# A two-layer hybrid backbone on one core: another order of the scan's preparation, the norms and the transposes of the mixed heads

## The reference

```
u = modulated_norm(x) @ w_in                 # partitioned into the head groups
ssd  = rmsnorm((y_f + flip(y_b) + xh * d) * silu(z))
hy   = order-2 long convolution
ml   = head_norm(h_f + flip(h_b)) * sigmoid(o)
x    = x + gate * (concat(ssd, hy, ml) @ w_out)
x    = x + gate * moe(modulated_norm(x))     # top group, then top 2 of its 8 experts
```

## Time and profile before

| | us |
|---|---|
| Runs | 1514.76, 1512.43, 1507.62 |
| Median | 1512.43 |
| The profiled execution's own time | 1514.76 |
| Its span in the trace | 1512.8 |

### The profile page before, as it was taken

One profiled execution on the slowest core, in us unless ns is written; L12 is line 12 of the kernel. 1 busy time (PEld: TensorE's weight loads), 2 busy tenths in 40 slices (PEclk: granted clock), 3 DMA queues, 4 the chain that ended last, 5 costly groups with the idle time before them and its releaser, 6 DMA issues. The chain is left out here.

```text
span 1512.8 us, 20013 instructions
## 1 busy us (share of the span) xinstructions
PE 1242.1 (82%) x7740; PEld 830.7 (55%) x7740; DVE 633.8 (42%) x1275; ACT 315.8 (21%) x622; POOL 128.2 (8%) x144
## 2 busy tenths in 40 slices
PE   5899999998889668899868449999879488888880
PEld 1544548987668544555434246568767355454450
DVE  4424862055792542333212164844474522222223
ACT  3202112243333201131101122122522111111111
POOL 0000000000000011212111000000000111211210
PEclk9999999998999779998979779999989599899896
DMA  9633232244430539999989455341532489999982
GB/s 284 190 112 112 74 101 70 91 148 135 137 115 29 195 124 375 396 365 363 378 285 388 177 192 186 112 125 43 195 117 73 183 323 393 376 386 376 375 334 88
DMA packets 157910, 322.19 MB, mean 213 GB/s; under 512 B 27963, under 2 KB 117112, under 8 KB 141176
## 3 DMA queue, kind: packets, MB, share of 16 engines
q1 hardware_dynamic: 146424, 305.12, 56.6%
q0 software_dynamic: 11392, 15.77, 3.3%
HBM read 321.11 MB, written 21.23 MB: 226 GB/s over the span
## 5 line engine op out<-in xcount | busy, mean ns | idle before, releaser
L533 PE MATMUL bank<-hT,ring 128*128 128x512 f32 (+1 forms) x544 | 203.6, 531 | 3.8 <-DVEq L1126 3.8
L533 PE MATMUL bank<-ring,qkT 128*64 128x256 f32 x1024 | 169.1, 426 | 38.0 <-DMA ring<-in_moe_w_up 26.5
L533 PE MATMUL bank<-ring,hT 128*128 128x256 f32 (+1 forms) x928 | 179.5, 348 | 2.4 <-DVE big L1544 1.5
L1544 DVE TENSOR_TENSOR xbc<-xbc,bank 64x256 f32<-64x256 f32 x65 | 27.5, 423 | 330.1 <-ACT xbc L1208 273.9
L533 PEld LDWEIGHTS bank<-ring,hT 128*128 128x128 f32 x928 | 154.0, 193 | 21.1 <-issue 3.3
L533 PEld LDWEIGHTS bank<-hT,ring 128*128 128x128 f32 x544 | 102.4, 190 | 99.3 <-issue 93.0
L533 PEld LDWEIGHTS bank<-ring,qkT 128*64 128x64 f32 x1024 | 107.1, 153 | 72.5 <-issue 34.9
L533 PE MATMUL bank<-hT,qkT 128*64 128x256 f32 x512 | 105.4, 440 | 28.9 <-DMA hT<-in_moe_w_up 19.9
L1141 POOL DMA_INDIRECT pair_rows<-hyT,zotok x65 | 60.1, 924 | 450.9 <-DVE xbc L1550 435.5
L1208 ACT ACTIVATE xbc<-bank 64x256 f32<-64x256 f32 x65 | 24.6, 378 | 312.0 <-PE bank L533 307.7
L533 PEld LDWEIGHTS bank<-hT,qkT 128*64 128x64 f32 x512 | 62.5, 159 | 47.3 <-issue 29.0
(11 more groups left out here) (285 smaller groups left out, 1719.8 us busy)
## 6 DMA issues: line engine op xcount, KB each, us to landing
ring<-in_w_mod SPq DMA_DIRECT2D x48, 1024.0 KB
ring<-in_moe_w_down SPq DMA_DIRECT2D x33, 1024.0 KB
ring<-in_moe_w_gate SPq DMA_DIRECT2D x32, 1024.0 KB
ring<-in_moe_w_up SPq DMA_DIRECT2D x32, 1024.0 KB
ring<-in_w_in SPq DMA_DIRECT2D x22, 1024.0 KB
hT<-in_moe_w_gate SPq DMA_DIRECT2D x16, 1024.0 KB
hT<-in_moe_w_up SPq DMA_DIRECT2D x16, 1024.0 KB
hT<-in_moe_w_down SPq DMA_DIRECT2D x16, 1024.0 KB
```

The source lines that it names most:

```text
L533: return nc.tensor.matmul(o, a, b, start=s, stop=e, **k)
L1544: step(V.tensor_tensor(o, a, b, op), *names)
```

## The change

Four things are reordered, and no arithmetic is added, removed or resized.

1. On VectorE, the turn of unit `u` was `scores(u + 1)`, `prep(u + 1)`, `combine(u)`, with unit 0's `prep` ahead of the loop. It is now `prep(u)`, `scores(u + 1)`, `combine(u)`: each `prep` moves from ahead of the `combine` of the unit before to behind it.
2. In layer 0, `mixed(0)` no longer interrupts the scan at unit 7 but follows it, on TensorE and on ScalarE. `head_squares(1)` moves from unit 7 to unit 6 and `gated_squares(1)` likewise; `mix_root(1)` stands ahead of `mixed(0)`.
3. In layer 0, ScalarE does `gated_squares` and `mix_root` of tiles 3 and 2 behind `mixed(0)`, `mixed(1)` and `gate_rows(0)`, each square followed by its root, and `mixed(3)` and `mixed(2)` behind tile 0's root of the second norm. VectorE finishes tile 3 up to its inverse before it begins tile 2. TensorE does `mixed(3)` and `mixed(2)` behind the first half of tile 1's projection instead of ahead of it.
4. In layer 1, `mixed(2)` stands behind `gate_rows(0)` and the whole projection of tile 3, on both engines.

```diff
# TensorE
-                    if (l, u) == (0, 7):
-                        mixed(0)
                     outputs_of(u)
...
-                if l:
-                    mixed(order[0])
+                mixed(order[0])
                 for n, t in enumerate(order):
                     b = product(("out", l, t, 0))
                     for q in range(2):
                         out_quarter(t, 0, q, b)
+                    if (l, n) == (0, 1):
+                        mixed(order[2])
+                        mixed(order[3])
                     if n:
                         normed_columns(order[n - 1])
                     elif l == 0:
...
                     out_quarter(t, 1, 0, b)
                     if n:
                         router(order[n - 1])
-                    elif l:
+                    out_quarter(t, 1, 1, b)
+                    if (l, n) == (1, 0):
+                        gate_rows(0)
                         mixed(order[1])
-                    out_quarter(t, 1, 1, b)
-                    if n == 0:
-                        if l == 0:
-                            mixed(order[2])
-                            mixed(order[3])
-                        else:
-                            gate_rows(0)
# ScalarE
-                    if (l, u) == (0, 7):
-                        mixed(0)
                         gated_squares(1)
-                        mix_root(1)
...
-                if l:
+                if l == 0:
+                    mix_root(1)
+                else:
                     gated_squares(3)
                     mix_root(3)
...
+                mixed(order[0])
                 if l == 0:
-                    for t in order[2:]:
-                        gated_squares(t)
-                    for t in order[2:]:
-                        mix_root(t)
                     mixed(order[1])
                     act.wait_ge(*due(("combined", l, len(units) - 1)))
                     gate_rows(0)
                     for t in order[2:]:
-                        mixed(t)
+                        gated_squares(t)
+                        mix_root(t)
                 else:
-                    mixed(order[0])
                     gated_squares(2)
                     mix_root(2)
-                    mixed(order[1])
                     act.wait_ge(*due(("combined", l, len(units) - 1)))
                     gate_rows(0)
+                    mixed(order[1])
                 for t in order:
...
+                    if (l, t) == (0, order[0]):
+                        mixed(order[2])
+                        mixed(order[3])
# VectorE
                 scores(0)
-                prep(0)
                 last_unit = len(units) - 1
                 for u in range(len(units)):
+                    prep(u)
                     if u < last_unit:
                         scores(u + 1)
...
                         gated(1)
+                        head_squares(1)
                         normed(0)
                     if l == 0 and u == last_unit:
-                        head_squares(1)
                         mix_inverse(1)
...
-                    if u < last_unit:
-                        prep(u + 1)
                     combine(u)
...
                     normed(1)
-                    for t in MIX_ORDER[l][2:]:
-                        gated(t)
-                        head_squares(t)
-                    for t in MIX_ORDER[l][2:]:
-                        mix_inverse(t)
-                    for t in MIX_ORDER[l][2:]:
-                        normed(t)
-                else:
-                    gated(2)
-                    head_squares(2)
-                    mix_inverse(2)
-                    normed(2)
+                    gated(3)
+                    head_squares(3)
+                    mix_inverse(3)
+                gated(2)
+                head_squares(2)
+                mix_inverse(2)
+                if l == 0:
+                    normed(3)
+                normed(2)
```

## The result

The changed kernel is slower: 1520.13 us median of eleven runs (1518.07 to 1524.32) beside 1510.32 for the kernel before (eleven runs, 1507.62 to 1518.98). The ratio is 1.0058, with an interval of 1.0041 to 1.0076, so 8.7 us where 6.0 the other way were forecast. Its profiled execution took 1515.24 us, less than any of its timed runs, so it is a lucky one. The kernel was run and profiled once more among the experiments, and I read both.

What follows compares the result with a forecast made beforehand. Weight DMA bounds the expert stages, untouched; in the scan VectorE and TensorE wait on each other in turn. Layer 0 1.2 us plus layer 1 4.8 early made 6.0, so 1506.4 us median; 8-in-10 range 1498 to 1515.

Steps and rivals of the forecast that it cites:

- unit 7's outputs: Layer 0, TensorE after about 9 us without work: 6.7 us, the middle between 4.4 at full clock and about 8.
- the router's wait: Layer 0, tile 0's router waits for ScalarE's h2 columns behind strided copies: 3.0 us lost, 0.8 more for the clock.
- the wait at the inverse: Layer 0, VectorE at mix_inverse(3) waits 6.7 us for ScalarE's square of tile 3, now behind copies and gate rows.
- 446.2 for the first bank read: Layer 0, VectorE's first read of an output bank: at 446.2 for 451.25, 5.0 us early.
- 7.3 less 2.4 in layer 1: Layer 1: out(3, 0) 7.3 us early, less 2.4 of TensorE waiting for ScalarE's copies before out(2, 0); 4.8 early.
- The scan: Layer 0's scan: rounds of 12.2 us for 15.5; VectorE ends unit 5's combine 17.7 us early.
- The third rival: Scan products at 1.2 GHz, each low spell costing 4.1 us, three spells: 1521.5 us; chance 0.08.
- What `head_squares(1)` costs: End of layer 0's scan, VectorE: head_squares(1) adds 2.5 us to the stretch before the last prep ends.
- the first rival: Tails eat the gain: low clock behind new waits, 2.8 us in layer 0, 1.7 in layer 1; 1510.9 us; chance 0.23.
- The rule that I weighed: TensorE is throttled by default until active, so unit 7's outputs take 8.0 for 6.7; 2.8 us later in layer 0.

Runs made afterwards that it cites:

- changed, again: The changed kernel, unaltered, timed and profiled a second time against the kernel before: +7.4 us, ratio 1.0049 (1.0028 to 1.0070).
- the idle matmuls: Changed kernel plus nine, later seven, unread matmuls of constants ahead of unit 7's outputs in layer 0: ratios to the kernel before 1.0045 and 1.0032.

## Why the prediction was wrong

Its places were right and its sum had the wrong sign. What failed is the price of the clock behind the waits that the change brings: unit 7's outputs were put at a middle value (6.7 us, measured 8.0), the clock behind the router's wait at 0.8 (measured 3.0 to 3.3), that at `out(2, 0)` in layer 1 at nothing (measured about 2), and the wait at the inverse was put too short (6.7, measured 7.8 and 9.5). Times from the start of each layer's scan:

| Step | before | forecast | changed | changed, again |
|---|---|---|---|---|
| unit 5's outputs | 87.6 | 73.6 | 72.0 | 75.2 |
| unit 7's outputs | 113.8 | 104.7 | 103.1 | 106.4 |
| out(0, 0) | 119.0 | 114.5 | 114.5 | 117.8 |
| first output bank read | 141.1 | 136.1 | 137.0 | 141.9 |
| router of tile 0 | 156.1 | 154.2 | 156.6 | 160.1 |
| tables of layer 0 | 226.0 | 224.8 | 229.8 | 233.0 |
| tables of layer 1 | 132.7 | 127.9 | 130.5 | 131.0 |

The prediction's 446.2 for the first bank read, beside 451.25, is the end of that read, so its start is put at 5.0 us ahead of before's. Its 7.3 less 2.4 in layer 1 is 4.9, not 4.8.

1. **The scan: right.** Rounds of 12.4 for 12.2 (369.26 to 381.62), and unit 5 within 1.6 us either way. What I had left out are the low spells with 0.6 us of idle or none ahead of them: 1.6 us each. The third rival spoke of such spells at 4.1 each; they do come, at less than half that price. Its 1521.5 lies near the measured 1520.13 by luck: its spells should have cost 12.3 us, and cost 3.2 in one profile of the changed kernel and nothing in the other.
2. **What `head_squares(1)` costs: right in place**, 2.4 measured for 2.5. That its cost brings a slow clock on top was not in the step.
3. **Unit 7's outputs, 6.7 us: wrong.** They took 7.7 to 8.0 in all nine profiles with a gap of 3.35 us or more ahead of them, and 4.2 with a gap of 1.15 or with the idle matmuls. Nothing lay between the two here, and the trace of before had the lower level behind 3.40 us of idle, which spoke for the whole price in place of the mean. In layer 1, behind 3.66 or 3.67 us, unit 7's outputs did take values between: 6.6 to 8.0 in the eleven profiles. In the repeat they begin at the full clock, and it falls 1.5 us into them. TensorE, layer 1:

```profile
1125.78 1.52 PE L533 MATMUL bank<-hfilt,big 128*128 128x64 f32 x12 [3.66 <-DVE big L1538]
1127.14 2.65 PE L533 MATMUL bank<-vaug,big 128*128 128x65 f32 x12
```

4. **The wait at the inverse, 6.7: right in the first profile but for 1.1** (7.84), 9.53 in the second. There the low clock runs on into `out(0, 0)`, whose first rows take 2.21 for 1.53, and since ScalarE's squares stand behind `mixed(1)`, every late matmul goes through ScalarE into VectorE. That made the first bank read 0.8 us later than before, for 5.0 earlier by forecast.
5. **Router of tile 0: the step that failed most in the first profile.** The wait of 3.1 us was forecast at 3.0, the clock behind it at 0.8. The stretch from there to the tables takes 73.2 and 72.9 for 69.9, so 3.0 to 3.3, and moving the copies back took it to 69.9. With `out(1, 0)`, 9.9 for 8.4 in the first profile, this is 4.0 of the 5.0 us by which layer 0 misses the forecast there (229.8 for 224.8); the bank read, 0.9 late, is the rest. In the second profile the miss is 8.2 us, and 5.8 of it are there by the bank read (141.9 for 136.1).
6. **Layer 1: the wait right (2.7 for 2.4), its clock left out of the forecast.** It was in the first rival at 1.7; the rows show 2.90 for 1.46 behind it, and from `out(2, 0)` to the tables it is 46.3 and 46.2 us for 44.3. Net 1.7 to 2.2 us early, for 4.8.

Together the terms 3 to 6 turn 6.0 us early into 1.6 late in the first profile (360.3 less 358.7), and with the spells and the longer wait into 5.1 late in the second (364.0 less the mean of 358.7 and 359.1). The timed 8.7 and 7.4 are 2 to 4 us more than the second; whether that is chance stays open. The first rival had the mechanism, the low clock behind each new wait, but priced it at 4.5 us in all, where the forecast missed the profiles by 7.6 and 11.1.

The rule that I weighed, in the Trainium skill (TensorE: Matmul & The Clock Gate, Part 1: The HAM clock gate), that activity releases a throttle which is there by default, agrees with the waits and with the idle matmuls: 8.0 us behind 5.97 of idle, 4.2 behind 6.28 of matmuls. Whether it covers the 3.52 us for `condp`, which stand behind matmuls of two columns and came in ten of the fourteen profiles, no run here shows.

The experiments go beyond the forecast in one thing: the moves of the tail are not a price for the scan's new order, as they cost 25.5 us without it. Taken back one at a time, squares 9.8, strided copies 6.5, layer 1 7.1 and `mixed(0)` 4.8 (the mean of 4.1 and 5.4) make 28 us, where together they gave 22. Each of these is known to 3 or 4 us, so that they add only in part is not shown.

## What to carry to other kernels

Change the order of the part that waits, and measure it before its neighbours are rearranged too: of the edits here one was worth 18 us, and the others together cost 25 to 27. An engine whose clock follows its work has two prices for an idle stretch, the stretch and the low clock behind it; where a forecast puts a gap of 3 us or more ahead of TensorE, it should price the rows behind at the lower level and not at a mean (unit 7's outputs, 4.2 us at the full clock, took 7.7 to 8.0 in layer 0 and 6.6 to 8.0 in layer 1). Work that is small and late on a third engine (here ScalarE's square of 0.5 us) belongs ahead of long copies that wait for TensorE, or it ties two engines that were free of each other.

## What the hardware showed

- Behind a gap of 3.08 to 3.12 us the router was slow every time (2.92 to 3.60 for 1.87, in eight profiles). Behind 2.69 in layer 1 six matmuls took from 1.53 to 2.90, and behind 1.15 and 1.75 in layer 0 nothing was lost.
- The length of the last gap alone doesn't tell. Behind 3.66 or 3.67 us in layer 1 the first twelve matmuls of unit 7's outputs took from 1.52 to 2.79 in eleven profiles, and where they took 1.52 the clock fell soon after. Behind 1.53 us the first six of `out(3, 0)` took 2.90.
- The lower clock came also in the scan with no idle ahead of it (3.52 for 1.93, behind 32 matmuls of two columns), in ten of the fourteen profiles. It makes identical stretches differ by 3.2 us from one execution to the next, so one profile each doesn't tell a change of that size.
